# Value products of an attention kernel: two heads at a time on alternating column halves

## The reference

```
s_b = (q_h . k_b) / 8          for b = selected, window, compressed, causal mask
p_b = softmax(s_b)
o_h = gate_c * p_c @ v_c + gate_s * p_s @ v_s + gate_w * p_w @ v_w
y   = sigmoid(mg0) * (rnn @ w_rg_out) + sigmoid(mg1) * (o @ w_nsa_out)
x   = x + y @ w_o
x   = x + (silu(rms(x) @ w_gate) * (rms(x) @ w_up)) @ w_down
```

## Time and profile before

| | |
|---|---|
| runs | 536.66, 537.23, 537.76 us; median 537.23 us |
| profiled execution, first to last instruction (span) | 535.1 us |
| time of the profiled execution beside its span | not recorded apart; the median of the runs is 2.1 us above the span |
| PE busy | 515.7 us, 96% of the span |
| PEld busy | 458.3 us, 86% |
| DVE busy | 317.4 us, 59% |
| ACT busy | 283.0 us, 53% |
| POOL busy | 56.2 us, 10% |
| mean granted TensorE clock | 0.981 of full |

### The profile page before, as it was taken

The page is one execution under the profiler, slowest core; times in us unless marked ns, Lnnn a source line. Parts: engine busy times, 40 slices in busy tenths (PEclk is TensorE's granted clock), DMA queues, the critical chain, the costliest instruction groups (busy, mean ns, idle before and its releaser), DMA issues.

```text
span 535.1 us, 8092 instructions
## 1 busy us (share of the span) xinstructions
PE 515.7 (96%) x3235; PEld 458.3 (86%) x3235; DVE 317.4 (59%) x418; ACT 283.0 (53%) x431; POOL 56.2 (10%) x93
## 2 busy tenths in 40 slices
PE   6999999699999889999999999799999999999997
PEld 6998998588989667777777788699999999988886
DVE  3999798799654654536464375654455455453432
ACT  5655978776357677564745343643533543543320
POOL 1000200940111322121211000000000000000000
PEclk9999999899799999999999999799999999999999
DMA  8645464625242224333623445064544555555502
GB/s 341 238 159 172 145 230 163 232 86 232 80 158 80 79 80 157 110 127 90 225 85 152 158 157 216 20 237 165 211 176 165 204 182 168 199 186 170 223 0 78
DMA packets 12546, 84.76 MB, mean 158 GB/s; under 512 B 1504, under 2 KB 1504, under 8 KB 2656
## 3 DMA queue, kind: packets, MB, share of 16 engines
q1 hardware_dynamic: 11808, 82.32, 42.3%
q0 software_dynamic: 272, 1.05, 0.6%
q10 hardware_dynamic: 432, 0.91, 0.4%
HBM read 83.22 MB, written 1.05 MB: 157 GB/s over the span
## 4 chain that ended last, share of the span: by engine, by line
PE 79%; issue 8%; ACT 4%; POOL 4%; DVE 3%; DMA 1%; POOLq 0%; DVEq 0%
PE bank L1035 23%; PE bank L1037 22%; PE bank L1036 22%; PE bank L1168 3%; PE bank L1132 2%; PE bank L1143 2%; POOL rs L311 2%; PE bank L1172 1%; PE bank L1170 1%; POOL pbuf L337 1%; DMA xs<-x_dram 1%; POOL scr L323 1%; ACT pbuf L428 1%; DVE w_lo L646 1%; PE bank L1133 1%
## 5 line engine op out<-in xcount | busy, mean ns | idle before, releaser
L646 DVE TENSOR_TENSOR w_lo<-raw,w_hi 128x2048 fp32r<-128x2048 f32 x77 | 179.2, 2331 | 125.7 <-ACT w_hi L359 125.3
L359 ACT ACTIVATE w_hi<-raw 128x2048 fp32r<-128x2048 f32 x77 | 147.3, 1918 | 116.5 <-PE bank L1037 115.7
L1035 PE MATMUL bank<-h_hi,w_hi 128*128 128x256 f32 x512 | 147.3, 288 | 1.0 <-DVE h_lo L693 1.0
L1036 PE MATMUL bank<-h_lo,w_hi 128*128 128x256 f32 x512 | 146.4, 286 | 0.0
L1037 PE MATMUL bank<-h_hi,w_lo 128*128 128x256 f32 x512 | 146.3, 286 | 0.0
L1035 PEld LDWEIGHTS bank<-h_hi,w_hi 128*128 128x128 f32 x512 | 99.9, 195 | 1.8 <-issue 1.6
L1036 PEld LDWEIGHTS bank<-h_lo,w_hi 128*128 128x128 f32 x512 | 99.9, 195 | 0.0
L1037 PEld LDWEIGHTS bank<-h_hi,w_lo 128*128 128x128 f32 x512 | 99.8, 195 | 0.0
L1035 PE MATMUL bank<-w_hi,act 128*128 128x512 f32 (+1 forms) x184 | 69.1, 376 | 0.0
L1037 PE MATMUL bank<-w_hi,act 128*128 128x512 f32 (+1 forms) x184 | 68.4, 372 | 0.0
L1036 PE MATMUL bank<-w_lo,act 128*128 128x512 f32 (+1 forms) x184 | 68.3, 371 | 0.0
(11 more groups left out here) (203 smaller groups left out, 551.0 us busy)
## 6 DMA issues: line engine op xcount, KB each, us to landing
raw<-stream_dram SPq DMA_DIRECT2D x77, 1024.0 KB, 4.8
xs<-x_dram POOLq DMA_DIRECT2D x1, 1024.0 KB, 5.5
out_dram<-xs SPq DMA_DIRECT2D x4, 256.0 KB, 2.0
xs<-x_dram ACTq DMA_DIRECT2D x1, 512.0 KB, 5.0
xs<-x_dram SPq DMA_DIRECT2D x1, 512.0 KB, 4.8
scr<-small_dram ACTq DMA_DIRECT2D x1, 320.0 KB, 10.2
prm<-params_dram ACTq DMA_DIRECT2D x1, 58.0 KB, 7.4
```

Of the source, the lines that this page charges most:

```text
L359: sc.activation(w_hi[:, i % HL, :], raw[:, i % RAW, :], ACT.Copy).then_inc(hi_ready, 1)
L646: ve.tensor_tensor(w_lo[:, i % HL, :], raw[:, i % RAW, :], f(w_hi[:, i % HL, :]), ALU.subtract).then_inc(lo_ready, 1)
L1035: pe.matmul(out_, l_hi, r_hi, start=start, stop=False)
L1036: pe.matmul(out_, l_hi, r_lo, start=False, stop=False)
```

## The change

`values` now takes a pair of heads and is called in every second slot, for `h` = 2, 4, ..., 16. The ten matmuls of the one head and the ten of the other are issued alternately, call by call, the even head to partitions 0 to 63 and the odd head to partitions 64 to 127. Each head of a pair has its own `pTa` and `pTb`, so `pbuf` is 768 columns wider. `o_done` counts pairs, and ScalarE's waits for it are counted and placed to match.

```diff
-        pbuf = sb("pbuf", [P, 1536])
+        pbuf = sb("pbuf", [P, 768 + 2 * 768])
...
-        pTa = pbuf[:, 768:1280]
-        pTb = pbuf[:, 1280:1536]
+        pTa = [pbuf[:, 768 + 768 * e:1280 + 768 * e] for e in range(2)]
+        pTb = [pbuf[:, 1280 + 768 * e:1536 + 768 * e] for e in range(2)]
...
                     pair = (h - 3) // 2
-                    sc.wait_ge(o_done, 2 * pair + 2)
+                    sc.wait_ge(o_done, pair + 1)
...
-                    if h >= 2:
-                        sc.wait_ge(o_done, h - 1)
-                    sc.activation(pTa, misc(m + 2)[:, :], ACT.Copy).then_inc(misc_free[(m + 2) % 4], 1)
+                    if h >= 3 and h % 2 == 1:
+                        sc.wait_ge(o_done, (h - 1) // 2)
+                    sc.activation(pTa[(h - 1) % 2], misc(m + 2)[:, :], ACT.Copy).then_inc(misc_free[(m + 2) % 4], 1)
...
-            def values(h):
-
-                g = h // (HEADS // GROUPS)
-                m = MISC["att"] + 4 * h + 2
-                o = o_bank[64 * (h % 2):64 * (h % 2) + 64, :]
-                wait_misc_read(pe, m)
-                wait_misc_read(pe, m + 1)
-                if h == 0:
+            def values(pair):
+
+                g = 2 * pair // (HEADS // GROUPS)
+                o = [o_bank[64 * e:64 * e + 64, :] for e in range(2)]
+                for e in range(2):
+                    m = MISC["att"] + 4 * (2 * pair + e) + 2
+                    wait_misc_read(pe, m)
+                    wait_misc_read(pe, m + 1)
+                if pair == 0:
...
                 for b in range(2):
-                    pe.matmul(o, v_sb[:, 0, b * S + g * DH:b * S + (g + 1) * DH], pTa[:, b * S:(b + 1) * S],
-                              start=b == 0, stop=False)
-                pe.matmul(o, vcx[:, h // 8, h % 8, :], pcT[:, h // 8, :], start=False, stop=True)
+                    for e in range(2):
+                        pe.matmul(o[e], v_sb[:, 0, b * S + g * DH:b * S + (g + 1) * DH], pTa[e][:, b * S:(b + 1) * S],
+                                  start=b == 0, stop=False)
+                for e in range(2):
+                    h = 2 * pair + e
+                    pe.matmul(o[e], vcx[:, h // 8, h % 8, :], pcT[:, h // 8, :], start=False, stop=True)
                 for b in range(2):
-                    ins = pe.matmul(o[:, P:S], v_sb[:, 1, b * S + g * DH:b * S + (g + 1) * DH], pTb[:, b * P:(b + 1) * P],
-                                    start=False, stop=True, skip_group_check=True)
+                    for e in range(2):
+                        ins = pe.matmul(o[e][:, P:S], v_sb[:, 1, b * S + g * DH:b * S + (g + 1) * DH], pTb[e][:, b * P:(b + 1) * P],
+                                        start=False, stop=True, skip_group_check=True)
                 ins.then_inc(o_done, 1)
...
-                if 1 <= h <= HEADS:
-                    values(h - 1)
+                if 2 <= h <= HEADS and h % 2 == 0:
+                    values(h // 2 - 1)
```

More of the change, by code:

```diff
@@ L407, in _ @@
                     sc.wait_ge(ta_done, h)
-                    if h >= 2:
-                        sc.wait_ge(o_done, h - 1)
-                    sc.activation(pTa, misc(m + 2)[:, :], ACT.Copy).then_inc(misc_free[(m + 2) % 4], 1)
+                    if h >= 3 and h % 2 == 1:
+                        sc.wait_ge(o_done, (h - 1) // 2)
+                    sc.activation(pTa[(h - 1) % 2], misc(m + 2)[:, :], ACT.Copy).then_inc(misc_free[(m + 2) % 4], 1)
                     sc.wait_ge(tb_done, h)
-                    sc.activation(pTb, misc(m + 3)[:, 0:256], ACT.Copy).then_inc(misc_free[(m + 3) % 4], 1)
+                    sc.activation(pTb[(h - 1) % 2], misc(m + 3)[:, 0:256], ACT.Copy).then_inc(misc_free[(m + 3) % 4], 1)
                 for v in range(2):
```

## The result

The changed kernel takes 528.56 us (median of 4 runs, 527.37 to 529.17), the kernel before 536.94 us (4 runs, 534.79 to 537.76). The ratio is 0.984, 95% interval 0.981 to 0.987: 8.4 us faster, where 2.8 us were forecast. The profiled execution took 529.17 us, with a span of 527.2 us, 7.9 us less than the span before; it was the slowest of the four runs, and so the spans differ by a little less than the medians.

A forecast was written before the change was run, and what follows sets the result against it. TensorE was taken to bound the kernel; -12.0 (odd slots) + 3.4 (even slots) + 5.8 (clock) = -2.8 us, span 535.1 to 532.3 us, giving 534.4 us with the median's 2.1 us offset; range 529.0 to 545.0.

The forecast's parts named there:

- Direction: Whole kernel: faster, by 2.8 us; chances 63% faster, 29% slower, 8% the same.
- bound: Attention stage: TensorE bounds it, so time taken off TensorE is time off the run, until something else becomes late.
- odd slots: Attention slots, numbered by the loop's h: 1, 7, 9, 11, 13, 15 each lose 2.0 us with their block, 12.0 us.
- Slots 3 and 5: Removed blocks give nothing there; TensorE's waits for GpSimd's scaled probabilities grow to 3.5 and 3.8 us.
- the extra of a pair: Even slots: a second head's products add 0.42 us to the block, 3.4 us over eight slots.
- floor: Even slots: least extra for a second head, 0.22 us, one half-step left over if the halves overlap.
- The clock: Longer waits in slots 3 and 5 each drop TensorE to half clock, costing 2.9 us each, 5.8 us for both.
- The second rival: Same as "The clock stays up"; it put the least idle time that drops the clock between 1.78 and 4.08 us.
- The halves do not overlap: Even slots: a pair's second head costs the full 1.73 us, 13.8 us in all; 544.8 us with both falls; 30%.
- The clock stays up: Slots 3 and 5: halves overlap and no clock fall comes, -8.6 us, 528.6 us; 7%.
- The chain behind the probabilities becomes the bound: Shortened odd slots: only 0.6 us left; 0.4 us lost in each of four slots gives 536.0 us; no chance given.
- no-fall case: Slots 3 and 5: neither wait drops the clock; 7% with overlap, 2% without; the range leaves about half out.

The follow-up runs named there:

- e1: Changed kernel with all five products of the even head issued before the odd head's five; 539.19 us, ratio 1.004 to the kernel before.
- e2: Changed kernel with the products alternating in twos: two even, two odd, one and one, two and two; 529.25 us, ratio 0.988.
- e5: Changed kernel with the products in the order three even, three odd, two and two; 531.14 us, ratio 0.990.
- e3: Changed kernel with 30 more transposes of a constant in each of slots 3 and 5, ahead of the wait for GpSimd; 524.16 us, ratio 0.977.
- e9: Kernel before, with only the last of the five value products issued in slots 3 and 5; 540.67 us, ratio 1.007.
- e7: Changed kernel with 15 constant transposes ahead of the wait in each of slots 3 and 5; 525.73 us, ratio 0.979.
- e6: e4 with VectorE's weight-split row (line 647) of slots 3 and 5 issued in the next slot, behind drain and maxima; 524.55 us, ratio 0.978.
- e4: Changed kernel with pairs' products one slot later (slots 3, 5, ..., 15 and 16), a third buffer pair, drains moved to match; 524.27 us, ratio 0.976.

## Why the prediction was wrong

**Direction, bound, odd slots: right.** TensorE bounds the stage, and a slot that loses its block gets shorter by 1.96 us (2.0 forecast). Slots 3 and 5 gave nothing, as said. With 0.06 us for each of the eight even slots (seen in 2 and 8 to 14), the removed blocks gave 5 x 1.96 + 1.34 + 8 x 0.06 = 11.6 us and not 12.0, since slot 1 gave only 1.34. The prediction took slot 1 for one without a wait, but TensorE waits there for VectorE in front of the second transposes. The timeline of PE in the kernel before, and then in the changed one:

```profile
149.02 0.44 PE L1153 MATMUL bank<-ident,pbuf 128*128 128x128 f32 x2 [0.66 <-DVE vcx L786]
...
149.20 0.44 PE L1153 MATMUL bank<-ident,pbuf 128*128 128x128 f32 x2 [1.29 <-DVE vcx L786]
```

This wait stands at the front of the slot, not where the block was. It grew by 0.6 us because the slot begins 0.45 us earlier and VectorE is 0.2 us later: what was gained ahead of the stage became wait.

**The step that failed: the extra of a pair.** The prediction put it at 0.42 us, with a floor of 0.22. It measured 0.01 us: 1.89 us for the block of two heads, 1.88 for that of one. (That even slots are 0.06 us shorter is the load exposed at the first transpose behind a block, which the prediction had counted into its 2.0 us.) The floor came from reading the order of the rows as binding: both rows of an even head's product first, then those of the odd head. The chip starts a matmul for the free half past up to three waiting ones for the busy half (e1, e2, e5), so no step and no load shows. This term was 3.4 us and measured 0.1: 3.3 us of the miss of 5.1 (-2.8 us forecast, -7.9 measured, in spans).

**The clock: right in kind, too large in size.** Both waits cost clock (e3, e9). The prediction took 2.9 us each; slots 4 and 6 are 1.54 and 2.62 us longer than the other even slots (9.04), 4.2 us in all, in place of 5.8: 1.6 us of the miss. The first stretch at half clock lasted 3.4 us, not the 6.8 of the three seen before. e7 and e9 show both lengths as well. The second rival's reading that the least idle time which costs clock lies between 1.78 and 4.08 us was not borne out by its own profile: the stretch at 340.8 has only 1.67 us ahead of it. The rest of the miss is 0.5 us outside the stage, whose cause is not known, less the 0.4 us that slot 1 did not give: 3.3 + 1.6 + 0.5 - 0.4 = 5.0 us.

**The rivals.** "The halves do not overlap" is false. "The clock stays up" is false, though its 528.6 us are where the time came out; it had 0.42 us a pair and no falls, where the chip had none of the one and 4.2 us of the other, and the two nearly cancel. e3, which is that case, took 524.2. "The chain behind the probabilities becomes the bound" does not hold in the changed kernel, where slots 7 to 15 take 7.14 us without a wait for GpSimd; it does in e6, where VectorE's long row holds GpSimd's last row up by 2 us. In e4 the wait is for the drain, another chain, which the prediction did not have as a rival.

The range was 529.0 to 545.0; the time lies just below it. Its lower end gave half of the no-fall case away, and nowhere did it hold an extra of zero.

What stays open: what idle time, after what work, costs clock (in slots 3 to 6 waits of up to 1.80 us did not and 2.03 us did; elsewhere 1.67 and 1.88 us did, though 1.67 not every time), what sets the length of a stretch at half clock, and what the reach of three counts.

## What to carry to other kernels

Two 64-column matmul chains that write different halves of the partitions cost TensorE here no more than one, if each product finds its partner within three waiting matmul rows; write them alternately, and don't issue one chain after the other. Work taken off the bounding engine in a place where it then waits is not only not gained: here each such wait cost 1.5 to 2.6 us more of TensorE's clock, so look first for the slots in which the engine waits already, and move work there. When VectorE's long row with two inputs in SBUF started just before a short GpSimd row, the short one took as long as the long one (e6): see which is first before a row is moved.

## What the runs showed of the hardware that was not expected

- Matmuls do not start in the order of the program when they go to different column halves: one started ahead of three earlier ones (e1, at 263.74), and with five waiting ahead of it, it started only when three were left (e5: slots 0.49 us longer).
- Full float32 products of 64 columns on both halves run at the full pace on each: eight rows in 1.08 us, as four before.
- Behind the start of the kernel, a stretch at half clock lasted 3.4 or 6.8 us in these profiles, but for one of 10.2 us ahead of the stage in e3.
- Transposes of a constant kept the clock at the full level through a wait of 3.4 us (e3), and behind 15 of them it stayed up once and fell once, with 1.75 and 2.03 us of the wait left (e7).
- A GpSimd row of 0.47 us took 2.51 us behind a VectorE row of 2.29 us that had started 0.13 us before it (e6).
